# Two-layer diffusion step: last expert's rows added by a one-hot product, and top-k in two halves

## Chip, cores and metric

One NeuronCore of a Trainium2 chip runs the whole step in one launch. The metric is the device time of one execution in microseconds (us); lower is better. The time before is the median of three runs.

## What is computed

Two trunk layers over 128 context tokens and 512 latent tokens, 1024 wide, in float32. A layer is a mixer (attention beside a state-space scan) and then an expert-choice channel mixer:

```python
x = x + g1 * jnp.dot(jnp.concatenate([attn, ssm], axis=-1), lp['w_out'])
h2 = rmsnorm(x, lp['norm2']) * (1 + sc2) + sh2
# expert_choice_ffn(h2), per set (context, latent)
aff = jax.nn.softmax(jnp.dot(xs, w_router).astype(jnp.float32), axis=-1)
cap = EC_FACTOR * n // N_EXPERTS              # 16 context, 64 latent
gates, idx = lax.top_k(aff.T, cap)
xe = xs[idx]
hid = jax.nn.silu(einsum(xe, w_gate)) * einsum(xe, w_up)
ye = einsum(hid, w_down) * gates[..., None]
out = jnp.zeros_like(xs).at[idx.reshape(-1)].add(ye.reshape(-1, D))
x = x + g2 * out
```

The next layer starts with `rmsnorm(x, norm1) * (1 + sc1) + sh1`, where the shifts and scales are the product of silu(c) with the layer's `ada_w` (the first modulation: its first 2048 columns).

## The kernel before

Tokens lie in five tiles of 128 (NT = 5; tile 0 is the context). Each engine has its own instruction list, written out by hand; semaphores, wrapped as `Signal`, order them. `arena` (SBUF) holds the weights: in the trunk the input projection (groups x0, x1, kv, q, z) and two slabs of the rest of the modulation, in the expert stage one expert's weights in six parts of 2 MB: 0 to 3 for gate and up, 4 and 5 for down. SP issues nearly all loads, in program order: a part is loaded when the product that read the part before it has signalled (`gu_used`, `dn_used`).

The expert stage of a layer is a loop over 16 experts. TensorE does for expert e: gate and up (`gate_up`), the turn of the next tokens (`tokens_in`), the down product of expert e - 1 (`down`), the turn of the hidden rows (`hidden`). So behind the loop one down product is left, that of expert 15 of the layer. VectorE closes an expert in `rows_out` (L1368 on): it waits until the scatter of the expert before has landed, since `idx_s` and `ys` are used again, takes the indices, and writes gate times g2 times the product into `ys`, 80 slots (64 latent, 16 context). GpSimd then adds the 80 rows into `x_res` in HBM by an indirect DMA (`scatter`, L1798) and notes its landing (`land`, L1805). Before that, GpSimd gathers the 80 token rows of a coming expert.

At the turn from layer 0 to layer 1 the order is this. SP, once the loop's loads are out: vectors, the four pieces of `ada_first` (L389), caches (k, v, router, eight state loads, L404), the two down parts of expert 15 (L449), the input groups (L410), and behind the load of x the slabs. TensorE: down of expert 15, the turn of the vector rows (L593), the first modulation (L603), the turn of its rows (L610), the 40 transposes of normed x (L528), and the trunk's products (L633), with a slab's product (L642) after each of the six chunks. ScalarE issues the load of x when the last scatter has landed, takes the squares (L1037); VectorE forms mean and norm (L1313, L1318), with the root on GpSimd (L1787).

The top-k (L1710 to L1731) works on affinities with an expert on each partition: latent tokens on partitions 0 to 15, context on 32 to 47, 512 columns. Eight rounds each take the eight largest values, replace them by -1 for the next round, and find their positions:

```python
link(V.max(topv[:, o], cur))
ins = V.match_replace(nxt, topv[:, o], cur, -1.0)
V.max_index(topu[:, o], topv[:, o], cur)
```

Values and positions are turned to one slot per partition (L1008), and the first gather follows.

## Time and profile before

| | |
|---|---|
| median of 3 runs | 1997.99 us (1995.8 to 2000.49) |
| profiled execution | 1995.96 us |
| its span in the profile | 1993.9 us |
| TensorE busy | 1824.8 us (92%) |
| VectorE, ScalarE, GpSimd busy | 655.1, 376.3, 201.0 us |
| HBM read, written | 503.91 MB, 24.38 MB |

The span is measured from the first to the last instruction of the profiled execution. Layer 0's trunk fills it up to about 420 us, its experts up to about 1000, and layer 1 the rest in the same order. PE is TensorE, PEld its weight loads, DVE VectorE, ACT ScalarE, POOL GpSimd, and a q behind a name is the DMA issue of that engine. A float32 product or turn leaves two matmul records in the trace.

### The profile page before, as it was taken

How to read it: one execution, taken by the hardware profiler on the slowest of the kernel's cores; microseconds unless marked ns; L12 is line 12 of the kernel's file. 1: busy time of each engine (PE TensorE's matmuls, PEld its weight loads, DVE VectorE, ACT ScalarE, POOL GpSimd, SP SyncE). 2: the span in 40 equal slices, each digit the busy share in tenths (PEclk: the TensorE clock that was granted, in tenths of full speed). 3: DMA queues.
4: the chain of work that ended last, by engine and by line, in shares of the span. 5: the costliest groups of instructions: out<-in, count | busy, mean ns of one | idle time of the engine just before them, and what ended most of it. 6: DMA issues, size and time to landing. Idle time of an engine off the chain costs nothing. (4 is left out here: it accounts for less than half of the span.)

```text
span 1993.9 us, 34559 instructions
## 1 busy us (share of the span) xinstructions
PE 1824.8 (92%) x14896; PEld 870.8 (44%) x14896; DVE 655.1 (33%) x1364; ACT 376.3 (19%) x896; POOL 201.0 (10%) x275
## 2 busy tenths in 40 slices
PE   4999989948999999999769999899399999999996
PEld 2465645422434343434334666454124344444443
DVE  2345875351212121212132557742502121221211
ACT  2224542110000010101022256321100000000000
POOL 1014200000000000001010231000001010101000
PEclk9999999978999999999879999999699999999998
DMA  9750022236999999999975301131279999999993
GB/s 386 279 216 1 6 99 112 87 119 244 389 393 408 399 404 404 405 407 403 375 277 196 127 1 61 43 138 74 112 295 387 403 395 405 397 411 397 411 395 103
DMA packets 56199, 526.48 MB, mean 264 GB/s; under 512 B 12046, under 2 KB 13694, under 8 KB 26142
## 3 DMA queue, kind: packets, MB, share of 16 engines
q1 hardware_dynamic: 48462, 498.81, 62.0%
q0 software_dynamic: 6336, 21.63, 4.5%
q10 hardware_dynamic: 1344, 5.24, 0.7%
q8 instruction: 40, 0.66, 0.1%
q14 instruction: 17, 0.14, 0.0%
HBM read 503.91 MB, written 24.38 MB: 265 GB/s over the span
## 5 line engine op out<-in xcount | busy, mean ns | idle before, releaser
L554 PE MATMUL PS<-arena,xe 128*32 128x512 f32 x6144 | 673.1, 598 | 3.8 <-DVE xe L1356 3.8
L554 PEld LDWEIGHTS PS<-arena,xe 128*32 128x32 f32 x6144 | 196.0, 111 | 457.5 <-issue 453.2
L578 PE MATMUL PS<-arena,hdT 128*32 128x512 f32 x1536 | 268.9, 600 | 13.2 <-DMA arena<-w_exp 11.2
L1367 DVE TENSOR_TENSOR RA<-RA,PS 96x512 f32<-96x512 f32 (+2 forms) x96 | 63.2, 684 | 648.7 <-ACT RA L1070 646.0
L580 PE MATMUL PS<-arena,hdT 128*32 128x256 f32 x1024 | 266.6, 383 | 0.0
L633 PE MATMUL PS<-arena,RB 128*128 128x512 f32 (+1 forms) x480 | 183.5, 530 | 0.0
L583 PE MATMUL PS<-arena,hdT 128*32 128x256 f32 x1536 | 156.9, 381 | 0.0
L584 PE MATMUL PS<-arena,hdT 128*32 128x256 f32 x512 | 153.3, 381 | 0.0
L1070 ACT ACTIVATE RA<-PS 96x512 f32<-96x512 f32 x32 | 19.0, 594 | 690.4 <-PE PS L554 690.4
L975 PE MATMUL PS<-arena,RB 128*128 128x512 f32 x320 | 138.9, 593 | 0.0
L580 PEld LDWEIGHTS PS<-arena,hdT 128*32 128x32 f32 x1024 | 110.9, 111 | 27.6 <-issue 1.0
L633 PEld LDWEIGHTS PS<-arena,RB 128*128 128x128 f32 x480 | 87.6, 190 | 68.6 <-issue 61.6
L633 PE MATMUL PS<-RB,arena 128*128 128x128 f32 (+1 forms) x384 | 106.8, 436 | 0.0
L1376 DVE SCALAR_TENSOR_TENSOR RA<-PS,gcur,RA 80x768 f32<-80x768 f32 x32 | 32.4, 1013 | 208.0 <-PE PS L584 208.0
L975 PEld LDWEIGHTS PS<-arena,RB 128*128 128x128 f32 x320 | 60.2, 190 | 73.0 <-issue 72.7
L1770 POOL TENSOR_TENSOR pgate<-pgate 128x1 f32<-128x1 f32 x66 | 12.5, 189 | 781.8 <-DVE idx_g L1342 444.1
L633 PEld LDWEIGHTS PS<-RB,arena 128*128 128x128 f32 x384 | 58.8, 191 | 54.5 <-issue 54.5
L578 PEld LDWEIGHTS PS<-arena,hdT 128*32 128x32 f32 x1536 | 60.8, 110 | 46.5 <-issue 12.1
L583 PEld LDWEIGHTS PS<-arena,hdT 128*32 128x32 f32 x1536 | 64.1, 111 | 33.8 <-issue 1.2
L1080 ACT ACTIVATE hdT<-PS 128x384 f32<-128x384 f32 x32 | 15.7, 490 | 316.5 <-PE PS L564 316.5
L1443 DVE SCALAR_TENSOR_TENSOR RF<-RE,vp,RF 128x644 f32<-128x644 f32 x48 | 42.7, 890 | 90.5 <-ACT RF L1133 89.2
L584 PEld LDWEIGHTS PS<-arena,hdT 128*32 128x32 f32 x512 | 56.7, 111 | 27.5 <-issue 0.8
(269 smaller groups left out, 1805.7 us busy)
## 6 DMA issues: line engine op xcount, KB each, us to landing
arena<-w_exp SPq DMA_DIRECT2D x192, 2048.0 KB, 12.9
arena<-ada_rest SPq DMA_DIRECT2D x16, 2048.0 KB, 7.6
ada<-ada_first SPq DMA_DIRECT2D x8, 2048.0 KB, 23.0
arena<-w_in SPq DMA_DIRECT2D x4, 2048.0 KB, 22.5
arena<-w_out SPq DMA_DIRECT2D x2, 4096.0 KB, 12.8
arena<-w_in SPq DMA_DIRECT2D x4, 1536.0 KB, 25.7
RC<-x_res SPq DMA_DIRECT2D x2, 2560.0 KB, 11.8
x_res<-RC SPq DMA_DIRECT2D x10, 512.0 KB, 2.6
```

Source lines behind the costliest of these rows:

```text
L554: last = mm(PS[GRP * q:GRP * (q + 1), c * 512:(c + 1) * 512], xe[:, k, GRP * grp:GRP * (grp + 1)], w[:, col_, :], start=(k == 0), stop=(k ...
L578: mm(PS[GRP * q:GRP * (q + 1), 1536:2048], tok(q), w[:, 0:512], start=first, **flags)
L580: mm(PS[96:P, 1536 + grp * REST:1536 + (grp + 1) * REST], tok(grp), w[:, MAIN:D], start=first and grp == 0, **flags)
L583: mm(PS[GRP * q:GRP * (q + 1), 2048:2304], tok(q), w[:, 512:MAIN], start=first, **flags)
L584: last = mm(PS[96:P, 2048:2304], tok(2), w[:, MAIN:D], start=first, **flags)
L633: last = mm(PS[:, o:o + width], lhs(k), rhs(k), start=(k == 0), stop=(k == KD - 1))
L975: last = mm(PS[:, o:o + 512], hT[:, k, t * P:(t + 1) * P], arena[:, w:w + 512], start=(k == 0), stop=(k == KD - 1))
L1070: A(hid[0:PAD, 0:512], PS[0:PAD, 0:512], ACT.Silu).then_inc(sg_rdy.sem, 1)
L1080: A(hdT[:, 0:4, :], low[:, :, 0:PAD], ACT.Copy)
L1367: V.tensor_tensor(h_, h_, up, ALU.mult).then_inc(hm_rdy.sem, 1)
L1376: V.scalar_tensor_tensor(ys[:, 0:MAIN], PS[0:SLOT, 1536:1536 + MAIN], gcur[0:SLOT, 0:1], g2r[:, 0:MAIN], ALU.mult, ALU.mult)
L1443: ins = V.scalar_tensor_tensor(cv[:, c, :], xin[:, c, w:w + CL], vp[:, r_:r_ + 1], cv[:, c, :], ALU.mult, ALU.add)
```

## The change

1. The last expert of layer 0. Its 80 rows reach the x of layer 1 without HBM: VectorE makes a table `oneh` (slot by token, 1 where the slot's index is the token) by comparing a row of numbers in PSUM with the slot's index; TensorE multiplies it with `ys`, five tiles of two products, in three PSUM places in turn; VectorE adds each tile to the x in SBUF. The scatter to `x_res` still runs, once x has been read; its landing is awaited later.
2. x is loaded by SP, when the last scatter but one has landed, into parts of `arena`; behind it SP waits for it to land before it goes on. Group x0 goes ahead, x1, the slabs, kv and the caches behind, and q and z behind the transposes of x, whose place they take.
3. Three pieces of `ada_first` go ahead of the last down parts, the fourth behind. The turn of the vector rows and half of the first modulation stand ahead of the last down product on TensorE, the other half behind it. ScalarE alone copies the modulation's rows in layer 1.
4. Top-k, both layers: the second half of the latent columns lies on partitions 64 to 79, all passes read 256 columns, and ten small operations join the two lists of 64: the first list against the second reversed, the larger of each pair.

```diff
+HROW = 64
+HALF = LAT // 2
...
-        wa = RE[0:CROW + EXP, 0:LAT]
-        wb = RE[0:CROW + EXP, LAT:2 * LAT]
-        topv = RE[0:CROW + EXP, 2 * LAT:2 * LAT + CAP_L]
+        wa = RE[0:HROW + EXP, 0:HALF]
+        wb = RE[0:HROW + EXP, HALF:2 * HALF]
+        topv = RE[0:HROW + EXP, 2 * HALF:2 * HALF + CAP_L]
+        mrg = RE[0:EXP, 2 * HALF + CAP_L:2 * HALF + 4 * CAP_L].rearrange("p (i c) -> p i c", i=3)
...
+        xs_early = [arena[:, t * D:(t + 1) * D] for t in range(4)] + [arena[:, W_Q:W_Q + D]]
+        oneh = arena[0:SLOT, W_Q + D:W_Q + D + TOK]
+        junk0 = arena[:, W_Q + 2 * D:W_Q + 3 * D]
...
+        def last_rows(t):
+
+            return (3072, 1024, 2048)[t % 3]
...
                 input_weights("x0", W_X, 3072)
+                if l:
+                    sp.wait_ge(landed.sem, landed.at(l, 0) - 1)
+                    sp.dma_start(arena[:, 0:4 * D].rearrange("p (t d) -> p t d", d=D), x_res[0:4 * P, :].rearrange("(t p) d -> p t d", p=P)
+                                 ).then_inc(x_in.sem, 16)
+                    sp.dma_start(xs_early[4], x_res[4 * P:TOK, :]).then_inc(x_in.sem, 16)
+                if l:
+                    sp.wait_ge(x_in.sem, x_in.at(l, 2))
                 input_weights("x1", W_X + 3072, 3072)
                 if l:
-                    input_weights("kv", W_K, KD * KV_DT)
-                    input_weights("z", W_Z, KD * 512)
-                    sp.wait_ge(x_in.sem, x_in.at(l, 2))
                     sp.wait_ge(dn_used.sem, dn_used.at(l, 0))
                     slab(0)
                     slab(1)
+                    input_weights("kv", W_K, KD * KV_DT)
+                    caches(l)
+                    sp.wait_ge(tg_ps.sem, tg_ps.at(l, 10))
                     input_weights("q", W_Q, KD * 512)
+                    input_weights("z", W_Z, KD * 512)
...
+                    if l:
+                        sp.wait_ge(landed.sem, landed.at(l, 0))
                     sp.dma_start(xr, x_res.rearrange("(t p) d -> p t d", p=P)).then_inc(x2_in.sem, 16)
...
                     vectors(l + 1)
-                    first_modulation(l + 1)
-                    caches(l + 1)
+                    first_modulation(l + 1, (0, 1, 2))
                 down_parts(l * EXP + EXP - 1)
+                if l + 1 < LAYERS:
+                    first_modulation(l + 1, (3,))
...
+            def last_rows_spread(l):
+
+                pe.wait_ge(oh_rdy.sem, oh_rdy.at(l - 1, 1))
+                for t in range(NT):
+                    if t >= 3:
+                        pe.wait_ge(x_add.sem, x_add.at(l - 1, t - 2))
+                    for h in range(2):
+                        o = last_rows(t) + 512 * h
+                        last = mm(PS[:, o:o + 512], oneh[:, t * P:(t + 1) * P], ys[:, h * 512:(h + 1) * 512], start=True, stop=True)
+                    last.then_inc(oh_ps.sem, 1)
+                    if t == 2:
+                        first_rows(l)
...
+                if l + 1 < LAYERS:
+                    vectors_turned(l + 1)
+                    mm(PS[:, 1024:1024 + P], ones[:, :], upto[:, :], start=True, stop=True).then_inc(iota_ps.sem, 1)
+                    first_modulation(l + 1, range(4))
                 down(l * EXP + EXP - 1)
+                if l + 1 < LAYERS:
+                    first_modulation(l + 1, range(4, KD))
                 pe.wait_ge(ys_rdy.sem, ys_rdy.at(l, EXP))
...
+            def last_slots(l):
+
+                dve.wait_ge(iota_ps.sem, iota_ps.at(l, 1))
+                for t in range(NT):
+                    ins = V.tensor_scalar(oneh[:, t * P:(t + 1) * P], PS[0:SLOT, 1024:1024 + P], float(t * P - 1), col[:, 1, EXP - 1:EXP],
+                                          ALU.add, ALU.is_equal)
+                ins.then_inc(oh_rdy.sem, 1)
...
+                def added(t):
+
+                    dve.wait_ge(oh_ps.sem, oh_ps.at(l - 1, t + 1))
+                    o = last_rows(t)
+                    V.tensor_tensor(xs_early[t], PS[:, o:o + D], xs_early[t], ALU.add).then_inc(x_add.sem, 1)
+
                 if l:
-                    first_rows()
-                    pads_cleared()
-                mean_eps(l, 0, 0, D)
-                for t in range(NT):
-                    if t + 1 < NT:
-                        mean_eps(l, 0, t + 1, D)
-                    normed(l, 0, t, x_t[:, t, :], x_t[:, t, :])
+                    dve.wait_ge(x_in.sem, x_in.at(l, 2))
+                    added(0)
+                    added(1)
+                    mean_eps(l, 0, 0, D)
+                    for t in range(NT):
+                        if t + 2 < NT:
+                            added(t + 2)
+                        if t == 2:
+                            first_rows()
+                            pads_cleared()
+                        if t + 1 < NT:
+                            mean_eps(l, 0, t + 1, D)
+                        normed(l, 0, t, xs_early[t], xs_early[t])
...
-                V.tensor_copy(wa[0:EXP, :], PS[0:EXP, CTX:TOK])
+                V.tensor_copy(wa[0:EXP, :], PS[0:EXP, CTX:CTX + HALF])
+                V.tensor_copy(wa[HROW:HROW + EXP, :], PS[0:EXP, CTX + HALF:TOK])
                 link(V.tensor_copy(wa[CROW:CROW + EXP, 0:CTX], PS[0:EXP, 0:CTX]))
...
-                for st, rows, a, n in ((1, 0, 0, CAP_L), (0, CROW, CAP_L, CAP_C)):
-                    V.tensor_copy(top[0:EXP, 0, a:a + n], topv[rows:rows + EXP, 0:n])
-                    ins = V.tensor_scalar(top[0:EXP, 1, a:a + n], topu[rows:rows + EXP, 0:n], float(CTX * st), None, ALU.add)
-                ins.then_inc(top_rdy.sem, 1)
+                V.tensor_copy(top[0:EXP, 0, CAP_L:SLOT], topv[CROW:CROW + EXP, 0:CAP_C])
+                V.tensor_scalar(top[0:EXP, 1, CAP_L:SLOT], topu[CROW:CROW + EXP, 0:CAP_C], 0.0, None, ALU.add)
+
+                far = mrg[:, 0, :]
+                first_of, take = mrg[:, 1, :], mrg[:, 2, :]
+                picked = top[0:EXP, 1, 0:CAP_L]
+                V.tensor_copy(far, topv[HROW:HROW + EXP, :][:, ::-1])
+                V.tensor_scalar(picked, topu[HROW:HROW + EXP, :][:, ::-1], float(CTX + HALF), None, ALU.add)
+                link(V.tensor_scalar(first_of, topu[0:EXP, :], float(CTX), None, ALU.add))
+                V.tensor_tensor(top[0:EXP, 0, 0:CAP_L], topv[0:EXP, :], far, ALU.max)
+                V.tensor_tensor(first_of, first_of, picked, ALU.subtract)
+                link(V.tensor_tensor(take, topv[0:EXP, :], far, ALU.is_ge))
+                link(V.tensor_tensor(take, take, first_of, ALU.mult))
+                V.tensor_tensor(picked, picked, take, ALU.add).then_inc(top_rdy.sem, 1)
...
+                if l + 1 < LAYERS:
+                    vectors_in(l + 1)
+                    last_slots(l)
                 rows_out(l, EXP - 1, l * EXP + EXP - 1)
...
+                if l + 1 < LAYERS:
+                    pool.wait_ge(x_in.sem, x_in.at(l + 1, 2))
                 scatter(l * EXP + EXP - 1, held.at(l, 2 * EXP))
                 pool.wait_ge(gathered.sem, gathered.at(l, EXP + 1))
-                land(l * EXP + EXP - 1)
+            land(LAYERS * EXP - 1)
```

What moves, in three places. SP at the turn (vr, vrows, ada_first: vectors and first modulation; ckv, wr, hst: caches; w_exp: down parts of expert 15; w_in: input groups; ada_rest: slabs; x_res: x). Before:

```order
L389 DMA ada<-ada_first 128x2x2048 x4
L394 DMA ckv<-cache_k 128x128
L395 DMA ckv<-cache_v 128x128
L396 DMA wr<-w_router 128x8x16
L404 DMA hst<-state 128x64 x8
L449 DMA arena<-w_exp 128x4096 x2
L410 DMA arena<-w_in 128x3072 x2
L410 DMA arena<-w_in 128x2176
L410 DMA arena<-w_in 128x4096
L415 DMA arena<-ada_rest 128x4096 x2
L410 DMA arena<-w_in 128x4096
```

and now:

```order
L404 DMA ada<-ada_first 128x2x2048 x3
L472 DMA arena<-w_exp 128x4096 x2
L404 DMA ada<-ada_first 128x2x2048
L425 DMA arena<-w_in 128x3072
L438 DMA arena<-x_res 128x4x1024
L440 DMA arena<-x_res 128x1024
L425 DMA arena<-w_in 128x3072
L430 DMA arena<-ada_rest 128x4096 x2
L425 DMA arena<-w_in 128x2176
L409 DMA ckv<-cache_k 128x128
L410 DMA ckv<-cache_v 128x128
L411 DMA wr<-w_router 128x8x16
```

The down parts move ahead of the caches and of the fourth piece, x comes behind the first input group, and the caches and two input groups stand behind the first slabs.

TensorE ahead of the last down product (RA with ident: the turn of hidden rows; arena with hdT: the down product). Before:

```order
L564 MATMUL PS<-ident,RA 128x128 x6
L1018 REGISTER_ALU
L1018 COMPARE_AND_BRANCH
L578 MATMUL PS<-arena,hdT 32x512 x3
L580 MATMUL PS<-arena,hdT 32x256 x2
L583 MATMUL PS<-arena,hdT 32x256 x3
```

and now:

```order
L629 MATMUL PS<-ident,RA 128x128 x6
L1070 REGISTER_ALU
L1070 COMPARE_AND_BRANCH
L547 MATMUL PS<-ident,vr 128x120
L1080 MATMUL PS<-upto,ones 128x128
L555 MATMUL PS<-ada,silc 2x512 x16
L643 MATMUL PS<-arena,hdT 32x512 x3
L645 MATMUL PS<-arena,hdT 32x256 x2
```

The vector rows, the row of numbers and half of the modulation have come in between. Behind the down product, before:

```order
L584 MATMUL PS<-arena,hdT 32x256
L593 MATMUL PS<-ident,vr 128x120
L603 MATMUL PS<-ada,silc 2x512 x32
L610 MATMUL PS<-ident,RF 128x128 x4
L528 MATMUL PS<-ident,RA 128x128 x40
```

and now:

```order
L649 MATMUL PS<-arena,hdT 32x256
L555 MATMUL PS<-ada,silc 2x512 x16
L577 MATMUL PS<-RA,arena 128x512 x6
L566 MATMUL PS<-ident,RF 128x128 x4
L577 MATMUL PS<-RA,arena 128x512 x4
L593 MATMUL PS<-ident,arena 128x128 x40
L685 MATMUL PS<-RB,arena 128x512 x8
```

The other half of the modulation is left there, and the ten products of the one-hot table (RA with arena: ys and oneh) stand around the turn of the modulation's rows, ahead of the transposes of x.

VectorE at the turn (vp: vector rows; RA from PS and gcur: ys; rs: means). Before:

```order
L1376 SCALAR_TENSOR_TENSOR RA<-PS,gcur,RA 80x768
L1380 SCALAR_TENSOR_TENSOR RA<-PS,gcur,RA 32x256 x2
L1380 SCALAR_TENSOR_TENSOR RA<-PS,gcur,RA 16x256
L1397 COPY vp<-PS 128x120
L1399 MEMSET RF 128x512
L1405 COPY RF<-PS 2x512 x2
L1410 TENSOR_TENSOR mod<-PS,vp 128x32
L1417 SCALAR_TENSOR_TENSOR amp<-mod,vp 128x16
L1421 MEMSET RE 128x6x2
L1422 MEMSET RE 128x6x4
L1423 MEMSET RE 128x6x2
L1313 TENSOR_SCALAR rs<-ss 128x1 x2
```

and now:

```order
L1852 COMPARE_AND_BRANCH
L1448 COPY vp<-PS 128x120
L1449 MEMSET RF 128x512
L1455 TENSOR_SCALAR arena<-PS,col 80x128 x5
L1403 TENSOR_SCALAR idx_s<-col 80x1
L1433 TENSOR_SCALAR gcur<-gall 128x3
L1437 SCALAR_TENSOR_TENSOR RA<-PS,gcur,RA 80x768
L1441 SCALAR_TENSOR_TENSOR RA<-PS,gcur,RA 32x256 x2
L1441 SCALAR_TENSOR_TENSOR RA<-PS,gcur,RA 16x256
L1503 TENSOR_TENSOR arena<-PS,arena 128x1024 x2
L1374 TENSOR_SCALAR rs<-ss 128x1
L1503 TENSOR_TENSOR arena<-PS,arena 128x1024
```

The vector rows and the five comparisons are ahead of the closing of expert 15; behind it come the adds of x, between the means.

## Rows read from the trace of the kernel before

**Rows 1.** Busy time of each engine by stage; then TensorE's clock, DMA share, GB/s.
```profile
426.00:454.00 28.00, 2.31 (x14) 1.37 (x11) 19.50 (x71) 3.19 (x5) 1.36 (x2) 0.53 0.09 31
900.00:920.00 20.00, 20.00 (x236) 9.37 (x228) 5.33 (x12) 1.06 (x5) 2.73 (x4) 1.00 1.01 391
986.00:991.00 5.00, 4.17 (x28) 2.08 (x32) 0.23 (x2) 0.00 (x0) 0.19 (x1) 0.50 1.00 418
1021.00:1033.00 12.00, 8.28 (x41) 7.87 (x42) 8.19 (x17) 7.32 (x14) 4.03 (x5) 0.54 1.00 427
1033.00:1096.00 63.00, 63.00 (x284) 31.01 (x286) 18.14 (x21) 13.82 (x23) 0.94 (x1) 1.00 0.47 180
```

**Rows 2.** TensorE's waits in the whole span: total, times, longest.
```profile
PE PS L1008 <- DVE top L1731: 35.3, 2, 17.6
...
PE PS L578 <- DMA arena<-w_exp: 11.2, 1, 11.2
```

**Rows 3.** Timeline of VectorE, top-k of the first layer: start, us, line.
```profile
426.40 0.68 DVE L1710 COPY RE<-PS 16x512 f32<-16x512 f32 x1 [0.81 <-PE PS L1004]
427.09 0.28 DVE L1711 COPY RE<-PS 16x128 f32<-16x128 f32 x1
427.42 0.68 DVE L1717 MAX8 RE<-RE 48x8 f32<-48x512 f32 x1
...
428.21 0.67 DVE L1720 MATCH_REPLACE8 RE<-RE 48x512 f32<-48x512 f32 x1
...
428.88 0.68 DVE L1721 FIND_INDEX8 topu<-RE 48x8 uint32<-48x512 f32 x1
...
443.40 0.18 DVE L1730 COPY top<-RE 16x64 f32<-16x64 f32 x1
...
443.78 0.15 DVE L1731 TENSOR_SCALAR top<-topu 16x16 f32<-16x16 uint32 x1
```

**Rows 4.** Timeline of SP at the turn of the layers.
```profile
955.74 21.83 SPq L404 DMA_DIRECT2D hst<-state  x8
977.61 0.91 SPq L449 DMA_DIRECT2D arena<-w_exp  x2
```

**Rows 5.** Issue and landing of L389 (ada_first) and L449 (from 977 us).
```profile
L389 SPq DMA_DIRECT2D ada<-ada_first x4: 469/492/7767, 943.9 to 945.4; - x4
...
DMA to landing us min/median/max: 17.8/24.5/31.5
...
DMA to landing us min/median/max: 9.1/11.4/13.7
```

**Rows 6.** Timelines of TensorE, GpSimd, VectorE and ScalarE at the turn.
```profile
964.24 0.63 PE L578 MATMUL PS<-arena,hdT 128*32 128x512 f32 x3
...
974.74 0.88 PE L564 MATMUL PS<-ident,RA 128*128 128x128 f32 x6
...
977.79 1.42 POOL L1798 DMA_INDIRECT x_res<-RA,idx_s  x1
...
988.09 0.19 POOL L1805 TENSOR_TENSOR pgate<-pgate 128x1 f32<-128x1 f32 x1 [8.87 <-DMA x_res<-RA,idx_s]
...
999.52 1.01 DVE L1376 SCALAR_TENSOR_TENSOR RA<-PS,gcur,RA 80x768 f32<-80x768 f32 x1 [10.98 <-PE PS L584]
...
1002.36 7.05 PE L603 MATMUL PS<-ada,silc 128*2 128x512 f32 x64
...
1018.56 1.03 ACT L1037 ACTIVATE PS<-RA 128x1024 f32<-128x1024 f32 x1 [6.57 <-DMA RA<-x_res]
...
1025.85 0.76 DVE L1318 TENSOR_SCALAR RA<-RA,rs 128x1024 f32<-128x1024 f32 x1 [0.44 <-POOL rs L1787]
...
1032.77 8.82 PE L633 MATMUL PS<-RB,arena 128*128 128x512 f32 x32
```

**Rows 7.** VectorE's groups by shape: busy us, mean ns.
```profile
L1689 DVE TENSOR_TENSOR RC<-RC,RF 128x1024 f32<-128x1024 f32 x10 | 12.2, 1224 | 0.3
```

**Rows 8.** DMA issues by line: median us to landing.
```profile
RA<-x_res ACTq DMA_DIRECT2D x1, 2048.0 KB, 8.3
```

More of the change, by code:

```diff
@@ L385, in vectors, with first_modulation @@
                 sp.dma_start(bp[:, :], row(bparams, l).to_broadcast([P, BCOLS])).then_inc(vec_in.sem, 16)
-            def first_modulation(l):
-                for i in range(4):
+            def first_modulation(l, pieces):
+                for i in pieces:
                     sp.dma_start(ada1[:, 2 * i:2 * i + 2, :],
@@ L516, in _, with vectors_turned, first_modulation, first_rows @@
             mm = nc.tensor.matmul
+            def vectors_turned(l):
+                pe.wait_ge(vec_in.sem, vec_in.at(l, 2))
+                nc.tensor.transpose(bank(0, VROWS), vr[0:VROWS, :], ident[0:VROWS, 0:VROWS]).then_inc(vec_ps.sem, 1)
+            def first_modulation(l, chunks):
+                for c in chunks:
+                    if c % 2 == 0:
+                        pe.wait_ge(ada_in[c // 2].sem, ada_in[c // 2].at(l, 1))
+                    for q in range(4):
+                        last = mm(PS[32 * q:32 * q + 2, 512:1024], silc[:, c, :], ada1[:, c, q * 512:(q + 1) * 512],
+                                  start=(c == 0), stop=(c == KD - 1), skip_group_check=True)
+                if c == KD - 1:
+                    last.then_inc(ada_used.sem, 1)
+            def first_rows(l):
+                pe.wait_ge(rows_act.sem, rows_act.at(l, 1))
+                if l == 0:
+                    pe.wait_ge(rows_dve.sem, rows_dve.at(l, 1))
+                for i in range(4):
+                    last = nc.tensor.transpose(PS[:, 512 + i * P:512 + (i + 1) * P], mrows[:, i * P:(i + 1) * P], ident[:, :])
+                last.then_inc(mod_ps.sem, 1)
+            def last_rows_spread(l):
[9 more added lines that the diff above has]
+                        first_rows(l)
             def transpose_groups(l):
@@ L1100, in rows_copied @@
                     act.wait_ge(rows0.sem, rows0.at(l, 1))
-                    for q in (0, 1):
+                    for q in range(4) if l else (0, 1):
                         last = A(mrows[32 * q:32 * q + 2, :], PS[32 * q:32 * q + 2, 512:1024], ACT.Copy)
```

73 lines of the change are left out of this document (41 added, 32 removed).

## The prediction, made before the changed kernel was run

> **What bounds the kernel now.** I read the windows by stage first [rows 1]. In the expert stage TensorE is busy for all of its 20 us at a granted clock of 1.00 while the DMA share is 1.01; in the trunk of the second layer (1033 to 1096 us) it is busy for all of 63 us at half that DMA load. So in both long stages TensorE sets the pace, and what moves their start moves the end. The other windows show where it does not: 426 to 454 us (2.3 us of work in 28) and the turn from one layer to the next. The list of TensorE's waits [rows 2] names the largest single ones: 17.6 us for the top-k, once in each layer, and 11.2 us for the last expert's down weights. The sums come from the timelines of these two places [rows 3, 4, 6]. Everything behind each place is moved rigidly, since TensorE has no slack there.
>
> **Top-k, in both layers.** Now eight rounds run over 512 columns: 8 MAX8, 7 MATCH_REPLACE8 and 8 FIND_INDEX8, 0.67 to 0.68 us each [rows 3], 23 passes in all. The change puts the far half of the latent columns on partitions 64 to 79, so that the same 23 passes read 256 columns. No row has one of these at another width. Bounds: nothing is saved per pass, if the time is fixed, or half of it (0.34), if it is all width. The nearest rows are the two copies from PSUM: 0.68 us at 16x512 and 0.28 at 16x128 [rows 3], 1.04 ns a column and 0.15 us fixed. A pass has the same 0.68 at the same width, so I take 256 x 1.04 = 0.267 us per pass, 6.1 us per layer. Against it: the copy of 512 becomes two of 256 (one more fixed part, 0.15), and the end grows from four small operations, 443.40 to 443.93 us, 0.53 in all [rows 3], to ten, four of them waiting for the one before. At 0.14 us for each unlinked one and 0.2 to 0.24 for a linked one (the four before span 0.53) that is 1.8, or 1.3 more. Net 6.1 - 0.15 - 1.3 = 4.7 us a layer, **9.4 us** for both. Bounds for both: a loss of 2.9 (nothing per pass) and a gain of 12.8 (0.34 per pass). The expert stage starts that much earlier; the gather, the turn of the slots and the first expert follow as before.
>
> **The last expert's down product.** The four pieces of ada_first are issued from 943.9 to 945.4 [rows 5], and SP then spends 21.8 us on the eight state loads, so that the down weights of expert 15 go out only at 977.6 [rows 4], although down 14 has read its first half at about 969.5 and ends at 974.7 [rows 6]. They land 9.1 and 13.7 us after their issue, at 986.7 and 991.8 [rows 5]; that is the wait of 11.2. The pieces land 17.8 to 31.5 us after issue [rows 5], the first at 961.7 and the fourth at 976.9: 5.1 us for each 2 MB, one after the other. The change issues three pieces, then the two down parts as soon as down 14 frees them, then the fourth piece. Third piece 971.8; part 0, issued 969.5, 976.9; part 1, issued 974.7, 982.0; fourth piece 987.1; the first w_in group (1.5 MB) 990.9. TensorE's new order is hidden(15) to 975.6, then the vector rows, the row of numbers and half of the first modulation. The whole modulation takes 7.05 us [rows 6], so half 3.5, and the two small ones some 0.7: done at 979.8. Down 15 then needs 10.4 us at full clock (964.24 to the hidden turn at 974.7), to 990.2, where it now ends just before VectorE's closing at 999.52 [rows 6]. Part 1 is wanted at 985.0 and is there. TensorE has no idle stretch before it, while now it starts down 15 at half clock, 0.50 from 986 to 991, after 11 idle us [rows 1]. The second half of the modulation ends at 993.7; its last chunks wait for 987.1, which costs nothing.
>
> **The rows of the last expert.** VectorE's closing of expert 15 waits for the landing of the scatter before it, 988.1 [rows 6], which I leave where it is, since its issue at 977.8 and the load on the queues stay. It takes 2.5 us (999.52 to 1002.05 now), so ys is ready at 992.8. The five comparisons that make the one-hot table (80x128 each, bounded by the 0.28 of the 16x128 copy and the 0.68 of 512 columns, so 1.4 to 3.4 us together) lie between the closing of expert 14 and 988.1, where VectorE idles for want of that landing; were they behind ys, they would cost their 1.4 to 3.4. ScalarE copies all four row groups where it copied two, 4 x 0.68 by the 16x512 copy, beside the spread. Spread: the modulation's eight chunks take 0.88 us per 512 columns, so a tile of two products takes 1.8: tiles 0 to 2 are in PSUM at 995.5, 997.2 and 999.0, and the row turns follow.
>
> **x on the queue.** The two x loads wait for the 988.1 landing instead of that of the last scatter, and go out on SP. Now the big one takes 8.3 us [rows 8], and the other's issue is some 0.4. Bounds for the landing: 997.1, if they run from their issue at 988.4, and 999.6, if they start behind the first w_in group at 990.9. The pieces of rows 5 land in the order of issue and 5.1 us apart, so I take **999.5**. The Trainium skill (DMA: Bandwidth & Descriptors, Queues, rings and completion order) says that each DMA engine reads a ring in order and goes round robin only between queues; by that rule x on SP's queue starts behind w_in, 999.6, and on its own queue, as now, nearer to 997.1 and to a sum 2.4 us better. Rows 5 agree with it for SP's queue. SP itself waits for x before it issues the second w_in group and the slabs. The trunk's six chunks fill the 63 us of 1033 to 1096 [rows 1], 10.5 each, 8.8 of it products of w_in [rows 6] and then a slab's; so a trunk from 1017.7 wants slab 0 at 1026.5, slab 1 at 1037 and the second w_in group, at the fourth chunk, at 1049. 1.5 + 4 MB at 5.1 us per 2 MB need 14 us from 999.5: covered. Moved behind them: kv, the caches, and, behind the turns of x, the q and z groups (4 MB, 10 us), with slab 2 behind these, landing at about 1035 where it is wanted at 1047. If that cover were gone, it would cost the difference once.
>
> **From x to the trunk.** Now: squares at 1018.56, last normed tile done at 1026.61, transposes, trunk at 1032.77 [rows 6]. New: VectorE does five adds of 1.22 (the add of a 128x1024 pair [rows 7]), five norms of 0.76 [rows 6], and ten small ones (five means, two of the modulation, three pads) at the 0.16 of the small copies [rows 3], with 0.5 for gaps: 6.1 + 3.8 + 2.1 = 12.0 us, from 999.5 to 1011.5. The squares and roots now bring five tiles in 7.3 us, 1018.56 to 1025.85 [rows 6], faster than that, and run beside it. GpSimd issues the last scatter (1.4 us) just before the first root, which can push the first norm by some 0.5 and lies within the gaps. The products of tiles 3 and 4 wait for adds 0 and 1 and are done by 1004. From the last norm on all is as before. Gain at the turn: 1026.6 - 1011.5 = **15.1 us**.
>
> **Sum.** 9.4 + 15.1 = 24.5 us off the profiled execution's 1995.96 (its span is 1993.9): 1971.5. The median of the runs shown, 1997.99, lies 2.0 above that execution, so 1973.5 in its terms. About 0.2%, 4 us, is what a measurement here can tell from no change.
>
> **Rivals.**
> - *x or the parts land late.* Scatter traffic beside them made part 0 need 9.1 us now where 5.1 is the rate. If x lands at 1003.5, the turn saves 11.1: 1977.5. If the down parts still come only with everything queued around them, so that down 15 ends at 997, the spread ends after x and the turn saves some 10: 1978.5. For it: the DMA share is 1.01 in the expert stage [rows 1]. Against it: the orderly landings. Chance 0.2.
> - *Top-k passes cost the same at half the width.* 15.1 - 2.9 = 12.2: 1985.8. Against it: the copies, with the same time at 512. Chance 0.05.
> - *More than I count.* The transposes before the trunk ran at a clock of 0.54 after an idle stretch (1021 to 1033 [rows 1]); after the products they may keep more of it. 32 of them took 6.1 us, at full clock up to half of that would go, and x may land at 997: 5 us more, 1968.5. Chance 0.15.
> - *Slower, through SP.* The caches stand ahead of q and z, and an eight-load group with small rows held SP for 21.8 us behind 8 MB of weights. If it holds SP to time T now, slab 2 lands at about T + 17. It is wanted at 1047, so T over 1030 delays the trunk, and the gain of the turn and the top-k is gone when the delay passes 24.5, T over 1055: a hold of 50 us or more. At T = 1062 the time is 2005. Against it: 7 MB lie ahead, 17 us. Chance 0.03.
> - *No change by over 0.2%* needs a mix of the second and the fourth, or a top-k merge that eats its gain and an x at 1012. Chance 0.02.
>
> **Numbers.** My own case has 0.55. Faster by over 0.2%: my case and the first three rivals, 0.95; the same 0.02; slower 0.03. The range 1966 to 1982 takes in late x, late parts, the merge at double its estimate (2.6 more), and the better case; outside lie the fixed-cost top-k and the slow ones, and half of the extremes.
>
> **What would show it.** Right: MAX8 at 48x512 becomes 80x256 with 0.41 us; TensorE's wait for the top-k falls from 17.6 to about 13; no wait of TensorE for down weights in layer 0's last expert; down 15 ends some 9 us sooner against expert 14; squares begin some 17 us sooner and the trunk 15. Wrong: passes near 0.68, a landing of x more than 12 us after its issue, a wait of TensorE for a slab, q or z in the second trunk, or one for the part in front of down 15.

## The result and the profile after

The changed kernel took 1974.72 us (median of 4 runs, 1971.74 to 1975.83) against 1996.89 for the kernel before on the same chips: ratio 0.9887, 95% interval 0.9869 to 0.9905, so 22.2 us less, where 24.5 were forecast: 1973.5 as a median, in a range of 1966 to 1982. The profiled execution took 1975.83 us with a span of 1974.1, 19.8 under the span before.

TensorE's waits in the whole span (total, times, longest), against [rows 2]:

```profile
PE PS L1060 <- DVE top L1834: 26.0, 2, 13.0
...
PE PS L643 <- DMA arena<-w_exp: 2.7, 2, 2.0
```

The wait for the top-k fell from 17.6 to 13.0 us in both layers, that for down weights from 11.2 to at most 2.0. The two waits for down weights that are left (2.0 and 0.7 us, at 1946.9 and 1954.6) lie in the last experts of layer 1, none at the turn.

VectorE's timeline in the top-k of the first layer (start, us, line), against [rows 3]:

```profile
426.47 0.41 DVE L1801 COPY RE<-PS 16x256 f32<-16x256 f32 x1 [0.81 <-PE PS L1056]
426.90 0.42 DVE L1802 COPY RE<-PS 16x256 f32<-16x256 f32 x1
...
427.65 0.42 DVE L1809 MAX8 RE<-RE 80x8 f32<-80x256 f32 x1
...
428.18 0.41 DVE L1812 MATCH_REPLACE8 RE<-RE 80x256 f32<-80x256 f32 x1
...
428.58 0.42 DVE L1813 FIND_INDEX8 topu<-RE 80x8 uint32<-80x256 f32 x1
...
439.17 0.21 DVE L1834 TENSOR_TENSOR top<-top,RE 16x64 f32<-16x64 f32 x1
```

A pass takes 0.41 to 0.42 us at 256 columns where it took 0.67 to 0.68 at 512. The ten operations of the join start at 437.64 and end at 439.38.

SP's timeline at the turn, against [rows 4]:

```profile
965.82 5.51 SPq L472 DMA_DIRECT2D arena<-w_exp  x2
971.38 0.43 SPq L404 DMA_DIRECT2D ada<-ada_first  x1
971.86 0.47 SPq L425 DMA_DIRECT2D arena<-w_in  x1
985.16 0.38 SPq L438 DMA_DIRECT2D arena<-x_res  x1
985.58 0.51 SPq L440 DMA_DIRECT2D arena<-x_res  x1
996.77 0.33 SPq L425 DMA_DIRECT2D arena<-w_in  x1
...
1000.28 17.77 SPq L419 DMA_DIRECT2D hst<-state  x8
1018.09 0.91 SPq L425 DMA_DIRECT2D arena<-w_in  x2
```

The last down parts go out at 965.8 and 971.0, as soon as down 14 frees them, and the state loads, which held SP for 21.8 us ahead of them, now hold it for 17.8 with nothing urgent behind. From issue to landing the down parts (first row; min and max are the two) and the small load of x (issued 985.58) took:

```profile
DMA to landing us min/median/max: 7.8/8.8/9.9
...
DMA to landing us min/median/max: 11.2/11.2/11.2
```

So the down parts were there at 973.6 and 980.9. The other loads by the same reckoning: the fourth piece (issued 971.4) at 986.8, the first w_in group (issued 971.9) at 990.5, the large load of x at 995.0 and the small one at 996.8.

The timelines of three engines at the turn (TensorE, then one row of GpSimd, then VectorE), against [rows 6]:

```profile
972.04 3.61 PE L555 MATMUL PS<-ada,silc 128*2 128x512 f32 x32
...
986.13 3.64 PE L555 MATMUL PS<-ada,silc 128*2 128x512 f32 x32
...
989.70 5.42 PE L577 MATMUL PS<-RA,arena 80*128 80x512 f32 x12
...
998.05 7.20 PE L577 MATMUL PS<-RA,arena 80*128 80x512 f32 x8 [2.50 <-DVE arena L1503]
...
1009.79 6.20 PE L593 MATMUL PS<-ident,arena 128*128 128x128 f32 x32 [0.95 <-DVE arena L1379]
...
1015.83 8.82 PE L685 MATMUL PS<-RB,arena 128*128 128x512 f32 x32
...
984.94 0.19 POOL L1910 TENSOR_TENSOR pgate<-pgate 128x1 f32<-128x1 f32 x1 [9.57 <-DMA x_res<-RA,idx_s]
...
974.53 1.38 DVE L1455 TENSOR_SCALAR arena<-PS,col 80x128 f32<-80x128 f32 x5
...
986.45 1.01 DVE L1437 SCALAR_TENSOR_TENSOR RA<-PS,gcur,RA 80x768 f32<-80x768 f32 x1 [1.06 <-PE PS L649]
...
996.77 2.36 DVE L1503 TENSOR_TENSOR arena<-PS,arena 128x1024 f32<-128x1024 f32 x2 [7.80 <-DMA arena<-x_res]
...
1001.87 1.23 DVE L1503 TENSOR_TENSOR arena<-PS,arena 128x1024 f32<-128x1024 f32 x1 [0.60 <-PE PS L577]
...
1005.29 1.23 DVE L1503 TENSOR_TENSOR arena<-PS,arena 128x1024 f32<-128x1024 f32 x1 [1.47 <-PE PS L577]
...
1008.16 1.58 DVE L1379 TENSOR_SCALAR arena<-arena,rs 128x1024 f32<-128x1024 f32 x2 [0.28 <-POOL rs L1892]
```

I measure the turn from VectorE's closing of expert 14 (L1437, before L1376) to the trunk's first product, which takes the top-k and the clock of the first experts out: 974.85 to 1032.77 before, **57.9 us**, and 971.00 to 1015.83 now, **44.8 us**, 13.1 less. Closing 15 begins 15.5 us behind closing 14 (24.7 before), the adds at 25.8, and the last norm ends at 38.7 (51.8 before). The brackets show what was not foreseen: VectorE waited 0.60 and 1.47 us for the products of tiles 3 and 4. These took 3.6 us a tile, twice what tiles 0 to 2 took (5.42 for three). The windows say why (TensorE busy, weight loads, VectorE, ScalarE, GpSimd; clock; DMA share; GB/s):

```profile
989.00:995.00 6.00, 6.00 (x21) 2.39 (x14) 0.00 (x0) 2.35 (x4) 0.00 (x0) 1.00 0.97 393
995.00:998.00 3.00, 0.55 (x5) 0.31 (x3) 1.23 (x2) 0.00 (x0) 1.04 (x2) 0.98 0.40 94
998.00:1005.00 7.00, 6.95 (x8) 2.52 (x8) 5.13 (x8) 4.60 (x8) 3.11 (x4) 0.50 0.92 337
```

After 2.5 idle us the granted clock is 0.50, the lower of its two levels.

### The profile page after: what moved, and what is told of

The parts are those of the page before. It is cut to its first block and busy times, and to the rows that moved or that the text cites. A ratio compares the mean times of both kernels' runs of the same rounds, so it can differ in the third digit from the quotient of the medians.

```text
span 1974.1 us, 34631 instructions
## 1 busy us (share of the span) xinstructions
PE 1836.3 (93%) x14918; PEld 874.7 (44%) x14918; DVE 651.0 (33%) x1386; ACT 377.4 (19%) x898; POOL 200.3 (10%) x275
## 5 line engine op out<-in xcount | busy, mean ns | idle before, releaser
L1437 DVE SCALAR_TENSOR_TENSOR RA<-PS,gcur,RA 80x768 f32<-80x768 f32 x32 | 32.4, 1013 | 198.4 <-PE PS L649 198.4
## 6 DMA issues: line engine op xcount, KB each, us to landing
arena<-w_in SPq DMA_DIRECT2D x4, 2048.0 KB, 10.3
```

Of the source, the lines that this page charges most:

```text
L1437: V.scalar_tensor_tensor(ys[:, 0:MAIN], PS[0:SLOT, 1536:1536 + MAIN], gcur[0:SLOT, 0:1], g2r[:, 0:MAIN], ALU.mult, ALU.mult)
```

## Experiments

Each time stands beside runs of the kernel before on the same chip. "Adds", "norm" and "turn" are microseconds behind closing 14: the first add, the end of the last norm, the trunk's first product. They come from one profiled execution each. How well they repeat can be read from kernels that have the same turn: after, turn_only and warm_experts have 44.8, 44.6 and 44.8, all_turn and all_warm 39.1 and 38.8; before and topk_only, however, 57.9 and 60.7. The medians are of 4 to 11 runs on several chips, so that rows are best compared by their ratios. No variant of the changed kernel has an interval clear of the changed kernel's own, but for turn_only; what sets them apart is the profile.

| run | median us | ratio to before (95%) | adds | norm | turn |
|---|---|---|---|---|---|
| before | 1996.89 | 1 | | 51.8 | 57.9 |
| after | 1974.72 | 0.9887 (0.9869 to 0.9905) | 25.8 | 38.7 | 44.8 |
| topk_only | 1988.70 | 0.9961 (0.9946 to 0.9975) | | 54.5 | 60.7 |
| turn_only | 1981.82 | 0.9929 (0.9915 to 0.9943) | 25.8 | 38.8 | 44.6 |
| late_down | 1978.94 | 0.9909 (0.9895 to 0.9924) | 32.1 | 44.0 | 50.3 |
| sp_only | 1992.79 | 0.9982 (0.9974 to 0.9991) | | 49.5 | 55.2 |
| four_places | 1971.88 | 0.9877 (0.9861 to 0.9892) | 25.9 | 36.6 | 42.1 |
| x_own | 1974.91 | 0.9895 (0.9880 to 0.9911) | 25.9 | 38.8 | 44.9 |
| x_first | 1971.52 | 0.9871 (0.9854 to 0.9888) | 23.6 | 34.3 | 40.7 |
| x_tiles | 1970.99 | 0.9869 (0.9854 to 0.9884) | 21.8 | 36.4 | 41.8 |
| warm_spread | 1976.03 | 0.9902 (0.9885 to 0.9918) | 26.3 | 37.0 | 42.3 |
| warm_experts | 1976.58 | 0.9901 (0.9884 to 0.9918) | 26.0 | 38.9 | 44.8 |
| all_turn | 1969.01 | 0.9867 (0.9849 to 0.9886) | 22.4 | 34.0 | 39.1 |
| all_warm | 1972.88 | 0.9878 (0.9858 to 0.9898) | 21.9 | 33.5 | 38.8 |

### The two halves of the change apart

topk_only is the kernel before with the lines of item 4 of the change; turn_only is the changed kernel with these lines taken back.

One of the lines that differ, of topk_only against before:

```diff
-        wa = RE[0:CROW + EXP, 0:LAT]
+        wa = RE[0:HROW + EXP, 0:HALF]
...
```

and of turn_only against the changed kernel:

```diff
-        wa = RE[0:HROW + EXP, 0:HALF]
+        wa = RE[0:CROW + EXP, 0:LAT]
...
```

Expected of topk_only:

> Only the top-k in halves, all else as before. Theory: each layer's top-k is on the path alone and gives 4.6 us, of which the slower clock at the start of the experts takes some back: TensorE's wait for top-k 17.6 to 13.0 twice, the turn of the layers (closing of expert 14 to the trunk's first product) stays 57.9 us, time 7.5 to 9.2 us under before. Rival (the shorter pause changes the clock and the loads, so that the gain grows or is lost behind the top-k): under 5 us, or over 11.

Expected of turn_only:

> The changed kernel with the top-k of before. Theory: the turn falls from 57.9 to 44.8 us as in the changed kernel, time 13 us under before; this and the top-k alone add up to the whole (22 us). Rival (the two parts interact through clock or queue): the sum of the two differs from 22 by more than 4.

The medians lie 8.4 and 15.3 us under the kernel before (1997.09 in their runs), where 7.5 to 9.2 and 13 were expected. The sum, 23.7, is the whole (22.2) within the intervals: the parts add. One thing was missed: in the profiled execution of topk_only (1991.3 us, 2.6 over its median) the turn is 60.7, not 57.9, since TensorE waited 14.8 us for the last down weights. SP's timeline of topk_only:

```profile
956.41 20.10 SPq L407 DMA_DIRECT2D hst<-state  x8
976.56 1.08 SPq L452 DMA_DIRECT2D arena<-w_exp  x2
```

The state loads are out, and the down parts go, 5.0 us behind closing 14 (971.61) there, 2.8 in the kernel before. The code of the turn is the same in both, so with caches ahead of them the down parts do not go out at the same time in every execution.

### The down parts, alone and undone

late_down undoes SP's order in the changed kernel; sp_only brings it alone into the kernel before (there the caches stand behind the slabs and the q group). Extracts of both differences:

late_down, against the changed kernel:

```diff
-                    caches(l)
...
-                    first_modulation(l + 1, (0, 1, 2))
+                    first_modulation(l + 1, (0, 1, 2, 3))
+                    caches(l + 1)
                 down_parts(l * EXP + EXP - 1)
-                if l + 1 < LAYERS:
-                    first_modulation(l + 1, (3,))
```

sp_only, against the kernel before:

```diff
+                    caches(l)
...
-                    first_modulation(l + 1)
-                    caches(l + 1)
+                    first_modulation(l + 1, (0, 1, 2))
                 down_parts(l * EXP + EXP - 1)
+                if l + 1 < LAYERS:
+                    first_modulation(l + 1, (3,))
```

Expected of late_down:

> The changed kernel, but with all four pieces of ada_first and the caches ahead of the last down parts on SP, as before. Theory: down 15 waits 11 us again, x is there by then, and the one-hot products wait for the rows: adds begin some 4 us later (29.8 us behind the closing of expert 14, not 25.8), turn 48 to 50 us, time 3 to 5 us over the changed kernel. Rival (the early down parts carry the gain, 9 of 13 us): turn 54, 9 over the changed kernel.

Expected of sp_only:

> The kernel before with SP's order alone: three pieces, the last down parts, the fourth piece, the caches behind the slabs; scatter and load of x as before. Theory: down 15 ends some 12 us sooner, but the closing waits for the scatter of expert 14, so rows are ready 9 to 10 us sooner, the last scatter and the load of x then run beside the w_in groups and lose 2 to 4 of it: turn 50 to 53 us, time 5 to 8 us under before. Rival (all that the early down gives reaches the trunk): turn 48. Rival (x is held by the full queues): turn 56 or more.

late_down: 4.2 us over the changed kernel, turn 50.3; the adds began 32.1 us behind closing 14, later than the 29.8 expected, so the order of SP is worth 5.5 us of the turn beside the one-hot rows. Up to 2.1 of these may be the scatter between executions that topk_only showed: closing 15 came at 26.8 there, and at 24.7 in the kernel before, with the same loads ahead of the down parts. sp_only: closing 15 moves from 24.7 to 17.5 us, 7.2 sooner, but the turn gains 2.7 and the time 4.3 (1.8 to 5.2 by its interval). That missed what was expected, a turn of 50 to 53 and 5 to 8 us; 55.2 lies next to the rival's 56. GpSimd's timeline of sp_only shows where the rest went:

```profile
995.58 1.40 POOL L1800 DMA_INDIRECT x_res<-RA,idx_s  x1
1006.79 0.19 POOL L1807 TENSOR_TENSOR pgate<-pgate 128x1 f32<-128x1 f32 x1 [9.81 <-issue]
```

The last scatter lands 11.2 us after its issue, with the input groups on the queues; before, it went out at 1002.47 and had landed by 1009.62, 7.2 us. That takes 4 of the 7.2 us. The two parts alone do not add up to both: together 13.1, SP's order alone 2.7, the rest alone 7.6 (57.9 to 50.3). The one-hot rows take the slow scatter off the path, and so the early down product comes to count in full. How much of the 2.8 between 10.3 and 13.1 is this, and how much scatter between executions, these runs do not tell.

### How x comes in

All three are against the changed kernel. x_own gives the two loads of x to ScalarE:

```diff
-                    sp.wait_ge(landed.sem, landed.at(l, 0) - 1)
-                    sp.dma_start(arena[:, 0:4 * D].rearrange("p (t d) -> p t d", d=D), x_res[0:4 * P, :].rearrange("(t p) d -> p t d", p=P)
-                                 ).then_inc(x_in.sem, 16)
-                    sp.dma_start(xs_early[4], x_res[4 * P:TOK, :]).then_inc(x_in.sem, 16)
...
+                    act.wait_ge(landed.sem, landed.at(l, 0) - 1)
+                    act.dma_start(arena[:, 0:4 * D].rearrange("p (t d) -> p t d", d=D), x_res[0:4 * P, :].rearrange("(t p) d -> p t d", p=P)
+                                 ).then_inc(x_in.sem, 16)
+                    act.dma_start(xs_early[4], x_res[4 * P:TOK, :]).then_inc(x_in.sem, 16)
```

x_first puts them ahead of the first w_in group:

```diff
-                input_weights("x0", W_X, 3072)
                 if l:
                     sp.wait_ge(landed.sem, landed.at(l, 0) - 1)
...
                     sp.dma_start(xs_early[4], x_res[4 * P:TOK, :]).then_inc(x_in.sem, 16)
+                input_weights("x0", W_X, 3072)
```

x_tiles leaves them behind it and makes five of them, with a semaphore each:

```diff
-                    sp.dma_start(arena[:, 0:4 * D].rearrange("p (t d) -> p t d", d=D), x_res[0:4 * P, :].rearrange("(t p) d -> p t d", p=P)
-                                 ).then_inc(x_in.sem, 16)
-                    sp.dma_start(xs_early[4], x_res[4 * P:TOK, :]).then_inc(x_in.sem, 16)
+                    for t in range(NT):
+                        sp.dma_start(xs_early[t], x_res[t * P:(t + 1) * P, :]).then_inc(x_tile[t], 16)
...
+                    dve.wait_ge(x_tile[t], 16)
...
-                    dve.wait_ge(x_in.sem, x_in.at(l, 2))
...
-                    pool.wait_ge(x_in.sem, x_in.at(l + 1, 2))
+                    for t in range(NT):
+                        pool.wait_ge(x_tile[t], 16)
```

Expected of x_own:

> The changed kernel with the two loads of x issued by ScalarE, on their own queue, all else the same. Theory (a queue is read in order, two queues share): x no longer stands behind the first w_in group, adds start at 23 to 24.5 instead of 25.8, turn 42.5 to 43.8. Rival (the bytes share the engines anyway and x gets half the rate): adds start at 26 or later, turn as before or worse.

Expected of x_first:

> The changed kernel with the first w_in group issued behind the two loads of x. Theory: x starts at its issue, 14.2 us behind the closing of expert 14, behind the fourth modulation piece only, and lands at 23 instead of 25.8; the w_in group lands by 28 and is wanted at 42: turn 42.3. Rival (the queue pauses while SP waits, and the trunk waits for w_in): a new wait of TensorE for w_in, turn 45 or more.

Expected of x_tiles:

> The changed kernel with x in five loads, each with its own signal, so that the first add needs one tile. Theory: tile 0 lands about 22, the five land some 1.3 us apart, faster than VectorE adds; adds start at 22.5, turn 41 to 42.5; tiles 3 and 4 still pay half clock. Rival (the adds are held by the products, not by x: tile 0 in PSUM at 20.5): same as theory at the start, but the chain stretches and the turn is 43.5 or more.

x_own missed. The loads went out at 984.1 and 984.5 and landed 10.9 and 12.4 us later, at 995.0 and 996.9, and the adds begin at 25.9, as with x on SP's queue. The trace shows why: from 984 to 997 the DMA engines moved 354 GB/s in both kernels, and the first w_in group landed at 991.4 instead of 990.5. The same bytes go through at the same rate, and x, larger than what is left of the group, is the last of them on either queue. That is the rival's reason (the bytes share the engines), and nearly its outcome (26 or later). x_first, which takes the group's bytes out from in front of x, hit the start (23.6 against 23 expected) and did more than expected: TensorE's pause before tile 3 shrank to 0.6 us, the clock stayed, and the products of tiles 3 and 4 took 3.70 us:

```profile
997.32 3.70 PE L577 MATMUL PS<-RA,arena 80*128 80x512 f32 x8 [0.60 <-DVE arena L1503]
```

Turn 40.7, where 42.3 was expected, and no wait for w_in. In x_tiles the first add starts at 21.8 (22.5 expected), now when the products of tile 0 are there and not when x is. TensorE did not pause before tile 3, and tiles 3 and 4 took 3.60 us, not the half clock that was expected. The gain of that was lost to an order nobody had looked at, on GpSimd and so on VectorE:

```profile
997.84 1.40 POOL L1904 DMA_INDIRECT x_res<-RA,idx_s  x1 [0.48 <-issue]
998.79 1.88 POOL L1893 TENSOR_TENSOR rs<-rs,mhalf 128x1 f32<-128x1 f32 x2
...
999.89 0.75 DVE L1380 TENSOR_SCALAR arena<-arena,rs 128x1024 f32<-128x1024 f32 x1 [2.96 <-POOL rs L1893]
```

GpSimd first waits for all of x, then issues the scatter, then takes the first root; the first norm waits 3.0 us for it. The turn, 41.8, lies in the 41 to 42.5 that were expected, but by luck: a cost that did not come was replaced by one that was not foreseen.

### The clock of tiles 3 and 4, and the places

four_places gives the five tiles places of their own as far as they are free:

```diff
-            return (3072, 1024, 2048)[t % 3]
+            return (3072, 1024, 2048, 0, 3072)[t]
...
-                    if t >= 3:
-                        pe.wait_ge(x_add.sem, x_add.at(l - 1, t - 2))
+                    if t == 3:
+                        pe.wait_ge(rows_act.sem, rows_act.at(l, 1))
+                    if t == 4:
+                        pe.wait_ge(x_add.sem, x_add.at(l - 1, 1))
...
-                    if t == 2:
-                        first_rows(l)
+                pe.wait_ge(x_add.sem, x_add.at(l - 1, 2))
+                first_rows(l)
```

warm_spread adds products behind first_rows(l) of the changed kernel:

```diff
                     if t == 2:
                         first_rows(l)
+                        for i in range(3):
+                            mm(PS[:, 0:512], oneh[:, i * P:(i + 1) * P], ys[:, 0:512], start=True, stop=True)
```

Expected of four_places:

> The changed kernel with four PSUM places: tile 3 goes to banks 0 and 1, tile 4 to the place of tile 0, the modulation's rows are turned behind them. Theory: in the changed kernel the products of tiles 3 and 4 start at half clock after a pause and hold VectorE's adds for 0.6 and 1.5 us; with tile 3 multiplied before x lands both pauses go: adds start 25.8 us behind the closing of expert 14 as before, the last norm ends at 36.7 (38.7 in the changed kernel), turn 42.8 (44.8), time 2 us less. Rival (VectorE's own pace or the roots set it): norm end and turn unchanged within 0.3.

Expected of warm_spread:

> The changed kernel with three products more, of no use to the result, behind the turn of the modulation's rows, so that TensorE does not pause before tile 3. Theory (the pause of 2.5 us costs tiles 3 and 4 the clock, not the wait itself): the products of tiles 3 and 4 run at full clock (3.6 to 3.7 us for both, not 7.2), the adds are not held, last norm at 36.7 instead of 38.7 behind the closing of expert 14, turn 42.8. Rival (the place, not the clock): tile 3 still starts when add 0 is done, products 7 us, turn 44.8.

Both move the last norm by 2, to 36.6 and 37.0, and the turn by 2.7 and 2.6; the turn gains a little more than the norm because the last 32 transposes took 5.60 and 5.38 us instead of 6.20, the clock being up again sooner. In warm_spread the places and their waits are those of the changed kernel and only the pause is filled; TensorE's timeline and windows there:

```profile
995.63 2.74 PE L582 MATMUL PS<-RA,arena 80*128 80x512 f32 x6
998.30 3.70 PE L577 MATMUL PS<-RA,arena 80*128 80x512 f32 x8
```

```profile
998.00:1002.00 4.00, 4.00 (x9) 1.44 (x8) 3.92 (x7) 3.45 (x6) 2.37 (x3) 1.00 0.97 335
```

So it was the clock after the pause, and not the wait for a place, that held the adds. In whole times four_places stands under the changed kernel (1971.9), with intervals that overlap; warm_spread's median, 1976.0, does not show its 2.6 us of turn, which is less than the runs differ among themselves.

### The clock of the first expert

The first gate and up of a layer took 22.79 and 23.04 us before and 23.35 and 23.59 in the profiled execution of the changed kernel: 1.1 us of the top-k's gain is lost there. warm_experts was to get it back:

```diff
                 pe.wait_ge(g2_rdy.sem, g2_rdy.at(l, 1))
+                for i in range(26):
+                    mm(PS[:, 0:P], ones[:, :], since[:, :], start=True, stop=True)
```

Expected of warm_experts:

> The changed kernel with 26 products of 128 columns, of no use to the result, while the first gather of a layer runs (6.7 us). Theory (what the top-k gained and lost again is TensorE's clock): the first gate and up of each layer takes 23.4 and 23.6 us now, its first 5 at half clock, and 20.6 to 21.2 with the clock up: time 4 to 6 us under the changed kernel. Rival (the first expert is held by its weights or tokens): time within 1 us of the changed kernel.

It missed. The added products took 8.20 us, more than the gather they should hide behind (6.7), and the clock did not stay; the windows of warm_experts:

```profile
446.00:450.00 4.00, 4.00 (x33) 4.00 (x33) 0.00 (x0) 0.00 (x0) 0.00 (x0) 0.87 0.18 60
450.00:454.00 4.00, 2.09 (x23) 1.43 (x25) 1.84 (x5) 0.00 (x0) 0.19 (x1) 0.98 0.00 0
454.00:458.00 4.00, 4.00 (x28) 1.04 (x24) 0.00 (x0) 0.00 (x0) 0.93 (x1) 0.59 0.30 82
```

From 454 to 458 the clock is 0.59 again, after the turn of the tokens and a pause of 1.9 us, and the first gate and up took 22.50 us in both layers, against 23.35 and 23.59. The time, 1976.58, is not under the changed kernel's. Nor are the 0.6 us a layer that I had put down to the shorter top-k a fixed price. Over the nine kernels with the halved top-k and no added products, the first gate and up took 22.1 to 23.7 us, 23.1 in the mean of the 18 layers (22.17 and 23.67 in late_down, 23.43 and 22.32 in x_tiles); over the three with the old top-k 22.8 to 23.1, 22.9 in the mean. It goes by the moment at which the clock comes up, 2.8 us after the first product in layer 0 of late_down and 5.1 in the changed kernel. So the loss is 0.2 us a layer in the mean and 0.6 in the profiled execution. Whether a clock held through to the first product would pay stays open: this run did not hold it.

### Put together

all_turn has x in five loads ahead of the first w_in group, four places, and the roots of layer 1 ahead of the last scatter; all_warm adds the 26 products.

GpSimd's lines of all_turn, beside those shown above:

```diff
                 if l + 1 < LAYERS:
                     for t in range(NT):
+                        root(l + 1, 0, t)
                         pool.wait_ge(x_tile[t], 16)
                 scatter(l * EXP + EXP - 1, held.at(l, 2 * EXP))
```

Expected of all_turn:

> x in five loads with a signal each, ahead of the first w_in group, four PSUM places, and the roots of layer 1 ahead of the last scatter on GpSimd (in the tiles run GpSimd waited for all of x and the scatter before its first root, and VectorE waited 3.0 us for that). Theory: adds start at 21.3, when the products of tile 0 are there, and follow the products 1.8 us apart; last norm at 32 to 33.5, turn 38 to 39 against 44.8 in the changed kernel, 41.8 with tiles and 40.7 with x first: time 6 us under the changed kernel. Rival (roots or squares set the pace now): turn 40 to 41.

Expected of all_warm:

> The run before plus the 26 products in each layer. Theory: both gains add, turn 38 to 39 and the first gate and up of each layer near 21 us: 10 to 12 us under the changed kernel, 1963 to 1966. Rival (one hides the other): under 8.

all_turn has a turn of 39.1 us, next to the 38 to 39 expected, and the lowest median of all, 1969.01, with a ratio to before of 0.9867; the changed kernel's was 0.9887, and the intervals overlap, so that it is better than the changed kernel is shown by the turn and not by the times. Its parts missed on both sides: the adds start at 22.4 instead of 21.3 and the last norm ends at 34.0 instead of 33.5 at most, while the last transposes took 5.22 us instead of the 6.20 of the changed kernel. The late start goes back to the last down product again: TensorE waited 1.70 us for the second of its weight parts, and closing 15 came at 17.0 instead of 15.5. all_warm has the same turn within 0.3 and 1972.88, where 1963 to 1966 was expected: the products give nothing back, as in warm_experts, and my sum of both fell.

## Why the prediction was right, and where it was off

- **Top-k, 4.7 us a layer.** Measured 4.6 in the wait (17.6 to 13.0). The pass was taken at 0.41 by the copies' slope, and is 0.41 to 0.42; the join takes 1.74 us, 1.8 forecast. The step from there to the end, "the expert stage starts that much earlier", fell short in the profiled execution: the first gate and up ran 0.6 us longer in each layer (0.2 in the mean of all the kernels here). topk_only gave 8.4 in all, against 9.4.
- **The last down product.** Closing 15 was forecast 15.4 us behind closing 14 and came at 15.5. The two parts were forecast at 2.1 and 7.2 us behind closing 14 and landed at 2.6 and 9.9 behind it (973.6 and 980.9 against 971.00); the second, 2.7 late, came just as it was wanted. TensorE's weight loads stood 0.60 us for it (to 980.94), its products some 0.1. The slack of 3 us that the prediction counted on (there at 982.0, wanted at 985.0) was gone.
- **x at 24.7 us behind closing 14** (999.5 less 974.85): 25.8, 1.1 late. That it is so near is in part luck, for two errors nearly cancel. The first w_in group, which x stands behind, was forecast at 16.1 us and landed at 19.5, 3.4 late. The DMA engines moved 260 GB/s from 965 to 969 us, when the tail of the third piece and the first down part (issued 965.8) were all that SP had out, and 307 from 978 to 982, when the scatter of expert 14 moved its rows, against 401 to 422 in between and after; the prediction had 5.1 us for every 2 MB (411) without a gap. That accounts for some 2.5 us, by an estimate from these rates. Behind the group, x then took 6.3 us (990.5 to 996.8) where the prediction counted 8.6: it set the 8.3 us from issue to landing of the old load of x behind the group, though its own 5.1 us per 2 MB give 6.4 for the 2.5 MB of x. The scatter of expert 14 landed at 13.9 instead of 13.2, but x was issued 5.3 us before the group ahead of it had landed, so that this did not set x's time. That x waits behind what is queued ahead on SP is right: x_first took 2.2 us off.
- **x on a queue of its own.** From the rule of the Trainium skill (DMA: Bandwidth & Descriptors, Queues, rings and completion order) that a DMA engine reads a ring in order and goes round robin only between queues, the prediction drew that x on its own queue would come up to 2.4 us sooner. x_own shows no gain (25.9). The rule is not refuted by that; what I drew from it was wrong. The engines moved 354 GB/s with one queue and with two, and x, the larger load, ended when all bytes were through, at the same time in both kernels. On SP's queue the rule and the trace agree: fourth piece, w_in and the two loads of x land in the order of issue, at 986.8, 990.5, 995.0 and 996.8.
- **From x to the last norm, 12.0 us.** It took 13.0. This is the term that was mis-sized: "the products of tiles 3 and 4 wait for adds 0 and 1 and are done by 1004" took full clock for granted. At half clock they took 7.2 us and VectorE waited 2.1 in all; with the pause filled or gone the chain takes 10.7 (26.3 to 37.0 in warm_spread; 25.9 to 36.6; 23.6 to 34.3), less than my 12.0. So here too a sum that was 1.3 too large hid part of a cost of 2.3 that was left out. The roots, which I had put beside the adds, did not hold it in the changed kernel (0.3).
- **The turn: 13.1 where 15.1 was forecast.** 1.1 from x and 1.0 from the chain. The clock's 1.1 at the first experts is added to that, and 0.7 at the last expert of layer 1, where 20.4 us of lead became 19.7 and TensorE waits 0.72 us for down weights that it did not wait for before. With the top-k's 0.2 that makes 4.1 of the 4.7 between 24.5 and the 19.8 of the spans. The rest, 0.6, lies between the end of the first gate and up of layer 1 and the first closing: 39.15 us before and 39.77 now, at a granted clock of 0.96 and 0.91.
- **The rivals.** None decided. x and the parts came late, but by 1.1 and 2.7 us and not by the 4 to 5 of the first rival. "More than I count" did not come: the clock fell to 0.50 before the products of tiles 3 and 4 and was still there at the transposes, of which the last 32 took 6.20 us against 6.26. SP was held 17.8 us by the state loads, not 50, and no slab or group was late. "Nothing per pass" fell with the first MAX8.

## What to carry to other kernels

When two late things meet at one point, moving either alone can show less than its share (2.7 and 7.6 us, against 13.1 for both here): read both paths to the meeting point before judging a step by its own run. A pause of TensorE can cost more than its length: behind 2.5 us of it, eight products took 7.2 us instead of 3.7. A product on the critical path is best computed before the data it meets arrives. A second queue brings a large load no sooner when the engines are busy with what is ahead of it; changing the order does. An early load helps only as far as every engine on the way takes it early: follow the in-order list of each of them, the idlest too.

## What was not expected of the hardware

- The clock fell to 0.50 after a pause of 2.5 us between products and stayed at 1.00 after one of 0.6 us (x_first) and one of 1.2 us (four_places), at about the same place. It also fell after a pause of 1.9 us in warm_experts, behind other work.
- Top-k passes (MAX8, MATCH_REPLACE8, FIND_INDEX8) take 0.41 to 0.42 us at 80 partitions and 256 columns and 0.67 to 0.68 at 48 and 512, the same as a copy of 16 partitions and that width: by these two points 1.02 ns a column and 0.16 us fixed.
- x on a queue of its own landed no sooner than behind another load on SP's queue: 996.9 and 996.8 us, with 354 GB/s moved in both.
- The 80-row scatter takes from 5.0 us (topk_only, expert 14, while SP was held) to 11.2 (sp_only, beside the input groups), from issue to the note of its landing.
